# Down-projection weight loads of a 32-expert decoder layer moved from SyncE's DMA queue to ScalarE's

## What is computed

```python
logits = (x @ w_router + b_router).astype(f32)
top_v, top_i = lax.top_k(logits, TOP_K)
...
def expert_step(acc, ep):
    w1, b1, w2, b2, g = ep
    hdn = x @ w1 + b1                       # w1: 1024 x 2048
    gt = jnp.minimum(hdn[:, :D_FF], SWIGLU_LIMIT)
    up = jnp.clip(hdn[:, D_FF:], -SWIGLU_LIMIT, SWIGLU_LIMIT)
    act = (up + 1.0) * gt * jax.nn.sigmoid(SWIGLU_ALPHA * gt)
    return acc + g[:, None] * (act @ w2 + b2), None      # w2: 1024 x 1024
```

## Time and profile before

| | us |
|---|---|
| runs shown | 1312.22, 1314.96, 1316.99 (median 1314.96) |
| profiled execution, whole | 1311.35 |
| its span in the trace | 1309.6 |
| mean granted TensorE clock | 0.97 |
| busy: TensorE matmul | 1174.1 (90%) |
| busy: VectorE, ScalarE, GpSimd | 353.8, 171.9, 95.4 |
| transfers | 438.56 MB, mean 335 GB/s over the span |

### The profile page before, as it was taken

One profiled execution on the slowest core, in us unless ns is written; L12 is line 12 of the kernel. 1 busy time (PEld: TensorE's weight loads), 2 busy tenths in 40 slices (PEclk: granted clock), 3 DMA queues, 4 the chain that ended last, 5 costly groups with the idle time before them and its releaser, 6 DMA issues.

```text
span 1309.6 us, 14918 instructions
## 1 busy us (share of the span) xinstructions
PE 1174.1 (90%) x5551; PEld 546.2 (42%) x5551; DVE 353.8 (27%) x693; ACT 171.9 (13%) x330; POOL 95.4 (7%) x211
## 2 busy tenths in 40 slices
PE   3997888999999999999899998999998999999875
PEld 2754566533433343334334333433343343334264
DVE  6799823212111111121211111111212111111133
ACT  2113322110011001010100100100011001100022
POOL 4674400000000000000000000000000000000000
PEclk9997889998999999999999999999999999997988
DMA  8413033299999999999999999999999999999600
GB/s 298 148 40 158 11 131 129 79 418 418 417 394 417 418 416 417 417 417 419 418 418 417 419 418 418 417 417 417 417 418 419 417 419 416 419 416 417 279 1 34
DMA packets 89189, 438.56 MB, mean 335 GB/s; under 512 B 13632, under 2 KB 16832, under 8 KB 55344
## 3 DMA queue, kind: packets, MB, share of 16 engines
q1 hardware_dynamic: 88528, 437.60, 82.2%
q10 hardware_dynamic: 624, 0.45, 0.1%
HBM read 436.65 MB, written 2.41 MB: 335 GB/s over the span
## 4 chain that ended last, share of the span: by engine, by line
PE 64%; DMA 12%; DVE 10%; SPq 7%; ACT 4%; issue 3%; ACTq 0%; DVEq 0%
PE ps L926 24%; PE ps L943 14%; DMA ring_up<-in_w_up_dram 11%; PE ps L910 7%; SPq L397 4%; SPq L404 3%; PE ps L804 2%; PE ps L1065 2%; PE ps L518 2%; PE ps L921 2%; PE ps L933 1%; ACT region L1258 1%; PE ps L598 1%; PE ps L869 1%; DVE region L1720 1%
## 5 line engine op out<-in xcount | busy, mean ns | idle before, releaser
L926 PE MATMUL ps<-ring_up,region 128*64 128x512 f32 x2112 | 463.5, 594 | 5.5 <-DMA ring_up<-in_w_up_dram 5.4
L926 PEld LDWEIGHTS ps<-ring_up,region 128*64 128x64 f32 x2112 | 147.3, 137 | 319.4 <-issue 296.9
L943 PE MATMUL ps<-ring_dn,region 128*64 128x512 f32 x1056 | 242.1, 612 | 22.7 <-ACT region L1258 22.7
L1716 DVE TENSOR_SCALAR region<-ps 128x512 f32<-128x512 f32 x33 | 22.8, 692 | 718.4 <-PE ps L926 718.4
L943 PEld LDWEIGHTS ps<-ring_dn,region 128*64 128x64 f32 x1056 | 74.7, 140 | 169.1 <-issue 138.3
L910 PE MATMUL ps<-region,n_tok 128*128 128x256 f32 (+1 forms) x384 | 95.8, 394 | 0.0
L1256 ACT ACTIVATE region<-region 128x512 f32<-128x512 f32 x33 | 20.8, 631 | 497.8 <-DVE region L1716 497.8
L869 PE MATMUL ps<-region 128*128 128x264 f32 (+1 forms) x272 | 69.4, 399 | 15.0 <-DVE fb L1711 12.4
L485 POOL COPY region<-kst 128x64 f32 (+1 forms) x33 | 7.9, 239 | 1020.5 <-PE ps L926 956.0
L910 PEld LDWEIGHTS ps<-region,n_tok 128*128 128x128 f32 (+1 forms) x384 | 67.3, 188 | 31.2 <-issue 24.2
L1268 ACT ACTIVATE region<-ps 64x512 f32<-64x512 f32 x66 | 39.1, 592 | 245.8 <-PE ps L943 245.4
(11 more groups left out here) (347 smaller groups left out, 823.5 us busy)
## 6 DMA issues: line engine op xcount, KB each, us to landing
ring_up<-in_w_up_dram SPq DMA_DIRECT2D x264, 1024.0 KB, 19.1
ring_dn<-in_w_down_dram SPq DMA_DIRECT2D x132, 1024.0 KB, 17.9
ring_up<-in_w_in_dram SPq DMA_DIRECT2D x4, 1280.0 KB, 10.5
ring_dn<-in_w_out_dram SPq DMA_DIRECT2D x1, 4096.0 KB, 25.4
ring_up<-in_w_ple_gate_dram SPq DMA_DIRECT2D x4, 1024.0 KB, 11.5
x_tok<-in_x_prompt_dram SPq DMA_DIRECT2D x2, 512.0 KB
ring_up<-in_w_glu_dram SPq DMA_DIRECT2D x1, 1024.0 KB, 15.3
region<-in_w_ple_proj_dram SPq DMA_DIRECT2D x1, 1024.0 KB
```

The source lines that it names most:

```text
L926: m = mm(ps[64 * (q % 2):64 * (q % 2) + 64, HID_B + q // 2, :], xe[:, k, slots], ring_up[:, k, q * 512:(q + 1) * 512], start=False, stop=( ...
L943: m = mm(ps[64 * half:64 * half + 64, OUT_B, :], act_t[:, f % 4, 64 * (f // 4):64 * (f // 4) + 64], ring_dn[:, f, 512 * half:512 * half + ...
```

## The change

The four down loads of each visit but the first leave SP's program. ScalarE issues them in load_down: behind outputs(t) of a visit it issues the four loads of visit t + 1. Expert 0's down loads stay on SP. The last quad is taken out of ScalarE's loop and written out behind it, since its last visit can't know the expert of a further visit; the further visit issues its own down loads at its start, with the expert read from the list. The up loads stay on SP, with the same waits.

```diff
@@ block.sync, expert() @@
                     sp.dma_start(ring_up[:, k], up_w[bass.ds(e, 1), k].rearrange("e p n -> (e p) n")
                                  ).then_inc(up_in[k], 16)
+                if not first:
+                    return
                 for s in range(DN):
-                    if first:
-                        sp.wait_ge(Z["mix_ps"], KD)
-                    else:
-                        sp.wait_ge(Z["dn_free"], t * DN + (s + 1 - DN))
-                    sp.dma_start(ring_dn[:, 2 * s:2 * s + 2], dn_w[bass.ds(e, 1), s].rearrange("e p k n -> (e p) k n")
-                                 ).then_inc(dn_in[s], 16)
+                    sp.wait_ge(Z["mix_ps"], KD)
+                    sp.dma_start(ring_dn[:, 2 * s:2 * s + 2], dn_w[0, s]).then_inc(dn_in[s], 16)
@@ block.scalar @@
-            with act.Fori(0, QUADS) as q:
+            def load_down(e, t):
+
+                for s in range(DN):
+                    act.wait_ge(Z["dn_free"], DN * t + (s + 1 - DN))
+                    act.dma_start(ring_dn[:, 2 * s:2 * s + 2], dn_w[bass.ds(e, 1), s].rearrange("e p k n -> (e p) k n")
+                                  ).then_inc(dn_in[s], 16)
+
+            def quad(q, place=None):
                 for a in range(2):
-                    activation(4 * q + 2 * a)
-                    outputs(4 * q + 2 * a, a, 0)
+                    t = 4 * q + 2 * a
+                    activation(t)
+                    outputs(t, a, 0)
+                    load_down(t + 1, t + 1)
                     selection(2 * q + a, a)
-                    activation(4 * q + 2 * a + 1)
-                    outputs(4 * q + 2 * a + 1, a, 1)
-
-            def visit(v, _):
+                    activation(t + 1)
+                    outputs(t + 1, a, 1)
+                    if place != "last" or a == 0:
+                        load_down(t + 2, t + 2)
+
+            with act.Fori(0, QUADS - 1) as q:
+                quad(q)
+            quad(QUADS - 1, "last")
+
+            def visit(v, e):
+                load_down(e, NE + v)
                 activation(NE + v)
                 outputs(NE + v, 0, 0)
                 selection(PAIRS + v, 0)
 
-            further_visits(act, visit)
+            further_visits(act, visit, expert_of=True)
```

More of the change, by code:

```diff
@@ L312, in powers @@
                                 [x.unsqueeze(2).to_broadcast([P, ST, k]) for x in step], sc_)
+        dn_w = A["w_down"][0].rearrange("e (s k p) n -> e s p k n", p=P, k=2)
         block = ctx.enter_context(nc.Block())
@@ L386, in _ @@
             up_w = A["w_up"][0].rearrange("e (k p) n -> e k p n", p=P)
-            dn_w = A["w_down"][0].rearrange("e (s k p) n -> e s p k n", p=P, k=2)
             def expert(e, t, first=False):
```

## The result

| | before | after |
|---|---|---|
| median of the runs | 1313.88 us (4 runs) | 1386.88 us (4 runs) |
| profiled execution's span | 1309.6 us | 1385.3 us |
| TensorE matmul busy | 1174.1 us | 1201.0 us |
| mean granted clock | 0.97 | 0.948 |

The ratio is 1.0553, 95% interval 1.0529 to 1.0576: slower by 73 us. The forecast was 1385, range 1328 to 1430. The size came out; the place did not quite, as the rows show.

The account below looks back on a forecast made before the run. TensorE sets the pace for some 15 experts, then the transfers at 418 GB/s. A 128.0 us cycle made down(31) 65.3 us later: 1311.4 + 65.3 + 5 (clock) = 1382, median 3.6 above: 1385 us, range 1328 to 1430.

Parts of the forecast that it names:

- The share: Up and down queues alternate single packets of any size: two thirds of bandwidth for up, one third for down.
- The order and the refill: Down slots refilled together after down ends, beside up(t+2) which is needed later; SP loses nothing but its four waits.
- The issue cost on ScalarE: Four down issues behind the output copies take ScalarE 1.8 us, covered by up(t+1) of 13.95 us: cost nothing.
- The sum by kinds: Times between ends of down for four kinds of expert: 30.3, 29.3, 32.7, 35.7 us, a cycle of 128.0 us.
- Between issue and first packet lies about 1.0 us: Start delay of a load's transfer, so down t+1 starts 1.5 us after the end of down(t).
- lockstep: Rival: down finds up active from its first packet in three of four experts; cycle 139.8, about 1480 us; chance 0.07.
- The signs: Expected in the profile: down waits up to 4 us in three of four experts, slices near 393 GB/s, median landing above 20.
- 27.6 us in all: TensorE's total wait before late up slots in the kernel before the change, as the prediction read it.
- The start and the clock: Down(0) ends at 277.76 us, as before; more falls of TensorE's clock add 5 us, from between 0 and 24.
- The rival of equal bytes: Both queues move equal bytes: no wait for down, up slowed, about 122 us a cycle, 1336 us; chance 0.18.
- No change: Rival: engines serve both queues in issue order, or ScalarE's issues block behind SP's; down lands before use; 1315 us; chance 0.06.
- faster: Rival: up's larger share removes waits before late up slots, down still lands within 22 us; at most 20 us, 1295; chance 0.03.

## Why the prediction was right, and where it was not

**The share** was right. One packet of each queue in turn, whatever its size, taken from 0.6 us of stores beside loads, held for deep queues at five pairs of sizes, down beside up: 4 and 8 KB, 8 and 8, 4 and 4, 2 and 8, 8 and 4. The Trainium skill (DMA: Bandwidth & Descriptors, "Queues, rings and completion order") has an engine drain a packet of 9 to 17 descriptors before it changes queues. Read as a load's whole share in turn, that would have given equal bytes for 4 beside 8 KB, two thirds for down with 4 KB each (where an up load is half as large), and a third with 2 KB beside 8. Measured for down were 1.53 MB of 4.14, 0.87 of 1.64 and 0.36 of 1.67; the measurement decides against it for these two queues. The pairs 8 and 8, 8 and 4 come out alike by both rules.

**The order and the refill** were right: single-queue lateness was priced at nothing and cost 3.5 us.

**The issue cost on ScalarE** was right: 128 issues at 380 ns. None took longer than 1.5 us. The selection copy came behind them as foreseen (16 times, 23.2 us in all), with nobody waiting for it yet. The first went out 0.26 us after the end of down (534.87 to 535.13), where 0.5 was taken; in the further visit it was 1.6, without a wait for it.

**The sum by kinds** was right in total and wrong in its parts. The text had 30.3, 29.3, 32.7 and 35.7 us, 128.0 a cycle; measured were 26.3, 37.2, 29.2 and 35.7, or 128.3 (129.4 over five cycles). The step that failed is "Between issue and first packet lies about 1.0 us", used for every expert. It holds only beside an idle queue. Beside one that is deep in work it is some 3.5 us, for SP's loads as for ScalarE's. The text had that for ScalarE's store at 174.77, but kept it for the upper bound, and never asked it of SP's refill. With it on both sides the parts come out: the first kind gets some 5 us alone and ends in time, the third does too (its loads, issued at 572.31, found an idle queue), and the second is the lockstep case, 0.26 + 3.5 + 30.1 + 1.3 + 3.7 for the last slot at the lower clock, or 38.9 against 37.2. The errors cancelled: two waits of 7.5 us together that did not come, and one that was 7.9 longer. That the cycle came out right is luck in this part.

**The signs.** As forecast: no wait for up, slices near 393 on the mean (390 from slice 9 to 37), SP waiting for the up matmuls alone, the longest landing of a down load 31.5 us, and no wait in the gather expert. Not as forecast: the median landing of the down loads was 13.3 us (page), not above 20, and the waits fell in the main into one expert of four, with up to 5.4 us each, not into three with up to 4. Both go back to the same step.

**"27.6 us in all"** for the waits for up was a misreading: the two rows overlap. TensorE's loss is better read from the length of up in the timeline, 16.07 instead of 13.95 us in the worst visits.

**The start and the clock.** Of the 75.7 us between the two spans 3.7 lie ahead of the end of down(0), 281.43 instead of 277.75, 2.7 of them because up(0) took 16.62 us instead of 13.95, the rest because it began 1.0 us later. A single-queue run without the change shows a late end there too (283.3 in the one with 8 KB pieces), and a two-queue run an early one (277.7 with 4 KB up pieces), so they are not its price. From down(0) to down(31) it is 1002.7 us against 930.6: +72, where +65.3 and 5 for the clock had been worked out.

**The rival of equal bytes** was priced at 1336, with 1.5 us of idle engines a cycle and a cycle of 122 us. Made real by equal pieces, it measured 1322, in cycles of about 120: below the lower end of the range that it had set. **No change** and **faster** found nothing in their favour, and **lockstep** came in one expert of four. Its "+94" is 90 by its own terms (7.4 us in experts 1 and 2, 82.6 in seven cycles), which changes nothing else.

## What to carry to other kernels

In these runs two DMA queues shared the engines packet by packet, so the queue with the smaller pieces got the smaller share. Before a load is moved to a second queue, work out when it is needed against that share, or make the pieces equal. Where the loads of one queue already stood in the order of use and the rate was at its limit, a second queue gave nothing (1319.23 against 1318.98 us) and cost up to 73. A late refill cost 3.5 us in a deep queue, and 65 (73 less 8) behind a small share.

## What was not expected of the hardware

- A queue that begins beside a working one comes in late, by some 3.5 us from the issue instead of about 1, in both directions. It does not go by the number of packets: 198 packets of 8 KB or 1.36 MB in the 3.2 us from 535.2 are matched in the kernel with 4 KB up pieces by 396 packets or 1.43 MB in the 3.5 us from 554.0 (first row), where ScalarE's first load, issued at 553.99, has moved nothing either. Nor is it a fixed time: where queue 1 had only 1.05 MB left, after the issue at 601.48, ScalarE's loads began when these were through, by 604.0, some 2.5 us later (second and third row). An estimate from these rows is that up to some 1.45 MB of the other queue, 3.5 us at 418 GB/s, go first; why stays open.

```profile
q1 hardware_dynamic: 396, 1.43, 102.5%
...
q1 hardware_dynamic: 145, 1.05, 100.0%
q10 hardware_dynamic: 1, 0.00, 0.4%
```

- The rate goes by the size of the pieces: 422 GB/s with all at 8 KB, 418 with two thirds of the bytes at 8 KB and the rest at 4 KB, 409 to 410 with all at 4 KB, 345 for 2 KB pieces alone.
- TensorE's clock fell once a cycle in the run with 8 KB pieces in one queue, with no wait for a transfer, and so took back what the faster transfers had given: 1.7 us in each of six cycles.
